# A PEER expert block: from one gathered and three dense token tiles to two and two, with dense products in plain f32

## What is computed

```python
qry = (h @ w_query).reshape(T, P_HEADS, 2, P_HALF)
scores = jnp.einsum("thcd,hcnd->thcn", qry, sub_keys).astype(jnp.float32)
s_top, i_top = lax.top_k(scores, P_TOPK)
...
gates = jax.nn.softmax(best_s, axis=-1).astype(h.dtype)
...
act = jax.nn.gelu(jnp.einsum("td,thkd->thk", hb, expert_u[eb]), approximate=False)
return jnp.einsum("thk,thkd->td", act * gb, expert_v[eb])
```

## Time and profile before

| | us |
|---|---|
| median of 3 runs | 1994.13 (1991.28 to 1994.95) |
| span of the profiled execution | 1990.5 |
| first u product | 822.9 |
| first fetch | 908.3 |
| u stage ends, v stage begins | about 1460 |
| last product | 1984.5 |

### The profile page before, as it was taken

One profiled execution on the slowest core, in us unless ns is written; L12 is line 12 of the kernel. 1 busy time (PEld: TensorE's weight loads), 2 busy tenths in 40 slices (PEclk: granted clock), 3 DMA queues, 4 the chain that ended last, 5 costly groups with the idle time before them and its releaser, 6 DMA issues.

```text
span 1990.5 us, 27945 instructions
## 1 busy us (share of the span) xinstructions
PE 1935.9 (97%) x10357; PEld 1710.3 (86%) x10357; DVE 1497.9 (75%) x2735; ACT 723.5 (36%) x1331; POOL 420.1 (21%) x231
## 2 busy tenths in 40 slices
PE   7999999999999999999999999999999999999998
PEld 4789777889877988999999999999988888888887
DVE  4776645364576537788889999996688898889986
ACT  4110233010351343343443444444444444444443
POOL 0333211444102023001111511111221222222210
PEclk9999999999999999999999999999999999999999
DMA  7235311353112432257668688888999999999993
GB/s 276 86 115 195 121 56 40 130 200 117 63 43 85 149 106 85 95 171 273 226 217 276 221 319 303 300 304 299 397 387 401 401 400 401 399 401 395 402 378 131
DMA packets 212644, 465.94 MB, mean 234 GB/s; under 512 B 15625, under 2 KB 157121, under 8 KB 193345
## 3 DMA queue, kind: packets, MB, share of 16 engines
q1 hardware_dynamic: 193408, 330.43, 47.7%
q0 software_dynamic: 18432, 134.23, 17.1%
q10 hardware_dynamic: 704, 0.04, 0.0%
HBM read 410.12 MB, written 54.53 MB: 233 GB/s over the span
## 4 chain that ended last, share of the span: by engine, by line
PE 43%; DMA 9%; DVE 4%; ACT 1%; issue 1%; SPq 1%; DVEq 0%; POOLq 0%; POOL 0%; ACTq 0%
PE xin_ps_u L2148 22%; PE xin_out L2192 16%; DMA experts_hot<-act_scratch 6%; PE xin_out L2170 4%; DMA con_raw<-in_expert_u 2%; DMA con_raw<-in_expert_v 1%; DVE over_v_vlo L2453 1%; DVE in_ulo L2304 1%; DVE experts_acc L1960 1%; SPq L2120 1%; DVE experts_rows L1941 1%; DVE xin_wt L2450 0%; ACT in_uhi L2221 0%; DVE xin_wlo L2455 0%; ACT L2263 0%
## 5 line engine op out<-in xcount | busy, mean ns | idle before, releaser
L1934 POOL DMA_INDIRECT experts_rows<-in_expert_rows,experts_idx x128 | 204.7, 1599 | 915.7 <-DVE experts_acc L1960 779.3
L2148 PE MATMUL xin_ps_u<-con_h_hi,in_uhi 128*128 128x384 f32 x1024 | 349.0, 341 | 11.3 <-DVE in_ulo L2304 9.1
L2148 PE MATMUL xin_ps_u<-con_h_hi,in_ulo 128*128 128x384 f32 x1024 | 343.3, 335 | 0.0
L2148 PE MATMUL xin_ps_u<-con_h_lo,in_uhi 128*128 128x384 f32 x1024 | 343.2, 335 | 0.0
L2192 PE MATMUL xin_out<-over_v_vhi,xin_whi 128*128 128x512 f32 x768 | 238.7, 389 | 2.3 <-DVE xin_wlo L2455 2.2
L2192 PE MATMUL xin_out<-over_v_vhi,xin_wlo 128*128 128x512 f32 x768 | 238.5, 389 | 0.0
L2192 PE MATMUL xin_out<-over_v_vlo,xin_whi 128*128 128x512 f32 x768 | 238.4, 389 | 0.0
L2304 DVE TENSOR_TENSOR in_ulo<-con_raw,in_uhi 128x1024 fp32r<-128x1024 f32 x127 | 155.2, 1222 | 81.2 <-ACT in_uhi L2221 78.7
L2148 PEld LDWEIGHTS xin_ps_u<-con_h_hi,in_uhi 128*128 128x128 f32 x1024 | 193.2, 189 | 15.6 <-DVE in_ulo L2304 13.0
L2148 PEld LDWEIGHTS xin_ps_u<-con_h_lo,in_uhi 128*128 128x128 f32 x1024 | 193.3, 189 | 0.0
L2148 PEld LDWEIGHTS xin_ps_u<-con_h_hi,in_ulo 128*128 128x128 f32 x1024 | 192.9, 188 | 0.0
(11 more groups left out here) (445 smaller groups left out, 3738.5 us busy)
## 6 DMA issues: line engine op xcount, KB each, us to landing
con_raw<-in_expert_u SPq DMA_DIRECT2D x128, 512.0 KB, 4.7
con_raw<-in_expert_v SPq DMA_DIRECT2D x128, 512.0 KB, 11.9
con_raw<-in_w_in SPq DMA_DIRECT2D x36, 1024.0 KB, 6.2
act_scratch<-in_act SPq DMA_DIRECT2D x128, 192.0 KB, 2.2
experts_hot<-act_scratch SPq DMA_DIRECT2D x128, 192.0 KB, 12.1
gate_scratch<-in_stage SPq DMA_DIRECT2D x12, 1024.0 KB, 7.2
gate_scratch<-over_s_stage SPq DMA_DIRECT2D x12, 1024.0 KB, 8.0
experts_hot<-gate_scratch SPq DMA_DIRECT2D x16, 768.0 KB, 14.0
```

Source lines behind the costliest of these rows:

```text
L1934: pool.indirect_dma_start(out=self.rows[:, r % ROWS, :], out_offset=None, in_=table, in_offset=at).then_inc(self.row_in[r % ROWS], 16)
L2148: mm = pe.matmul(ps_u[s % 2][:, 0:TD], a[s % 2][:, k, :], m[:, k, P:T], start=(i == 0), stop=(i == 3 * KD - 1))
```

## The change

It removes the dense work of tile 1 and gathers that tile too: 256 slots, first those of tile 0 and then of tile 1, with the same four row buffers. The dense part has tiles 2 and 3 (256 tokens).

- The dense products are plain f32: no rounded parts, no cuts on ACT and DVE, 8 matmuls of 256 columns in a u step (L2139), 4 of 512 in a v step (L2176).
- Activations and gates stay on the chip in `w` (128 KB in each partition). In 64 u steps from `S0` = 54 on, four tokens' gates are made in each: DVE makes one-hot rows times gate (`weighted_rows`), ACT the other one-hot rows from a distance (`distances`, `one_hot`), PE four products of 128 columns (L2159). Blocks still to come are filled by ACT (`keep_gates`), those that are done are multiplied by DVE (`gate_done_tiles`, L2424), and `gate_tile` (L2432) multiplies the new block's.
- Slot r is now `slot_work(r)`: the dot product of r, then the add of r-2. Slots start at step 18, two in three steps up to S0, one in each step after it. 98 are done in the u stage. The other 158 follow one another on DVE with no tie to PE's steps, the routing of tile 1 between the first twelve.
- The v stage reads `w` and the loaded block alone.
- Before it, `finish_block` also turns h of tile 1 back to rows and stores two row tiles to HBM; the v stage's first loads bring them back, and the residual rows with them.

The core of the diff; the helpers for routing only take other buffers:

```diff
-                for r in IN_AT[n - 1] if n else []:
-                    got.add(dve, r)
-                for r in IN_AT[n]:
-                    got.dot(dve, r, con.h0[:])
...
+def slots_of_steps():
+    at, r = [[] for n in range(NEXP)], 0
+    for n in range(FIRST_SLOT, NEXP):
+        if n >= S0 or (n - FIRST_SLOT) % 3 != 2:
+            at[n].append(r)
+            r += 1
+    return at
...
     def fetch(self, pool, r, table):
 
-        at = bass.IndirectOffsetOnAxis(ap=self.idx[:, r:r + 1], axis=0)
+        g, c = r // SLOTS, r % SLOTS
+        if c == 0:
+            pool.wait_ge(self.idx_done, g + 1)
+        at = bass.IndirectOffsetOnAxis(ap=self.idx[g][:, c:c + 1], axis=0)
         wait(pool, self.acc_done, r - ROWS + 1)
...
+            def products(n):
+                pe.wait_ge(ring.u_in[n % U_RING], 16 * (n // U_RING + 1))
+
+                wait(pe, gelu_done, n - 3)
+                wait(pe, w_in_place, placed(n - 4))
                 for k in range(KD):
-                    for a, m in ((uhi, hT[0]), (uhi, hT[1]), (ulo, hT[0])):
...
+                    mm = pe.matmul(ps_u[n % 4][:, 0:TD], u_of[n % U_RING][:, k, :], con.late[:, k, :], start=(k == 0),
+                                   stop=(k == KD - 1))
...
+            for n in range(NEXP):
+                pe.wait_ge(ring.v_in[n % U_RING], 16 * (n // U_RING + 1))
+                wait(pe, w_in_place, placed(n))
+                for t in range(ND):
+                    for h in range(2):
+                        mm = pe.matmul(out[t][h][:], w[:, n, t * P:(t + 1) * P], ring.tile[n % U_RING][:, h * 512:(h + 1) * 512],
+                                       start=(n == 0), stop=(n == NEXP - 1))
...
+            def weighted_rows(q):
+
+                dve.wait_ge(slots_done, 1 if q < N_HOT // 2 else 2)
+                wait(dve, g_done, q - 1)
+                for k in range(G_TOK):
+                    c = G_TOK * q + k
+                    op = dve.tensor_scalar(hot_i[q % 2][:, k, :], con.iota[:], slot[0][:, c:c + 1], slot[2][:, c:c + 1],
+                                           ALU.is_equal, ALU.mult)
+                op.then_inc(hot_i_done, 1)
...
+            def slot_work(r):
+                if r == SLOTS:
+                    dve.wait_ge(h1_in, 16)
+                got.dot(dve, r, rows_of(r))
+                if r == SLOTS + 2:
+                    dve.wait_ge(v_used, 12)
+                if r > 1:
+                    got.add(dve, r - 2)
...
+            for n in range(NEXP):
...
+                if group_of(n + 1) is not None:
+                    weighted_rows(group_of(n + 1))
+                if n > S0:
+                    gate_tile(n - 1)
+                for r in IN_AT[n]:
+                    slot_work(r)
+                if group_of(n) is not None:
+                    gate_done_tiles(group_of(n), n)
+            gate_tile(NEXP - 1)
+            for r in range(AFTER, 2 * SLOTS):
+                slot_work(r)
+                if r - AFTER < R_STEPS:
+                    route(3, r - AFTER)
```

More of the change, by code:

```diff
@@ L1531, in modulate, with keep_h @@
                                    bias=con.ada[:, 24 + k:25 + k], scale=con.scale_b[:, k:k + 1]).then_inc(modded, 1)
+            def keep_h(dst, t, half):
+                act.wait_ge(back, 2 * t + half + 1)
+                act.activation(dst[:, half * 512:(half + 1) * 512], ps_x[:], ACT.Copy).then_inc(h0_kept, 1)
             act.wait_ge(landed[1], base + 16)
@@ L1555, in _ @@
                     half = i - U + 3
-                    act.wait_ge(back, half + 1)
-                    act.activation(con.h0[:, half * 512:(half + 1) * 512], ps_x[:], ACT.Copy).then_inc(h0_kept, 1)
+                    keep_h(con.h0, 0, half)
             modulate(2)
+            act.wait_ge(ss2_done, NT - 1)
+            for half in range(2):
+                keep_h(h1, 1, half)
             square_tile(3)
@@ L1898, in _ @@
                     keep_scores(g - 1)
-                if g == PH - 2:
-                    act.wait_ge(ring.u_in[0], 16)
-                    act.activation(uhi[0][:], ring.tile[0].rearrange("p (k n) -> p k n", k=KD), ACT.Copy).then_inc(cut_hi, 1)
             keep_scores(PH - 1)
@@ new lines, in _ @@
+            sp.wait_ge(rt.searched, PH)
+            sp.dma_start(lists1, rt.lists[1]).then_inc(away, 16)
+            for n in range(U_RING, NEXP):
+                sp.wait_ge(u_done, n - 3)
+                ring.load_u(sp, A, n)
+            for n in range(NEXP):
+                if n < U_RING:
+                    sp.wait_ge(u_done, NEXP - 3 + n)
+                else:
+                    sp.wait_ge(v_used, n - 3)
+                ring.load_v(sp, A, n)
+                if n == 5:
+                    sp.dma_start(again, lists1).then_inc(again_in, 16)
+                if n == 11:
+                    sp.dma_start(h1, kept_rows[1]).then_inc(h1_in, 16)
+                if n == 19:
+                    sp.dma_start(row_b, kept_rows[0]).then_inc(row_b_in, 16)
+                if n >= 27 and n % 4 == 3 and n < 27 + 4 * NT:
+                    t = (n - 27) // 4
@@ new lines, in gates @@
+            def gates(q):
+                pe.wait_ge(hot_j_done, q + 1)
+                pe.wait_ge(hot_i_done, q + 1)
+                wait(pe, g_in_place, q - 1)
+                for k in range(G_TOK):
+                    mm = pe.matmul(ps_g[q % 2][:, k, :], hot_j[q % 2][:, k, :], hot_i[q % 2][:, k, :], start=True, stop=True)
+                mm.then_inc(g_done, 1)
+            for n in range(NEXP):
+                if group_of(n) is not None:
+                    gates(group_of(n))
+                products(n)
+                if n in (S0 - 4, S0 - 2):
+                    turn_slots(1 + (n - S0 + 4) // 2)
@@ new lines, in distances, with one_hot @@
+            def distances(q):
+                act.wait_ge(slots_done, 1 if q < N_HOT // 2 else 2)
+                wait(act, hot_j_done, q)
+                for k in range(G_TOK):
+                    c = G_TOK * q + k
+                    op = act.activation(distance[:, k, :], con.iota[:], ACT.Abs, bias=slot[1][:, c:c + 1], scale=-1.0)
+                op.then_inc(measured, 1)
+            def one_hot(q):
+                act.wait_ge(measured, q + 1)
+                wait(act, g_done, q - 1)
+                act.activation(hot_j[q % 2], distance, ACT.Relu, bias=con.ones[:, 0:1], scale=-1.0).then_inc(hot_j_done, 1)
@@ new lines, in square @@
+            def square(g):
+                act.wait_ge(got.acc_done, SLOTS * (g + 1))
+                act.wait_ge(v_used, 20)
+                wait(act, ss0_done, g)
+                act.activation(junk, got.acc[g], ACT.Square, accum_out=ss0[:, g:g + 1]).then_inc(ss0_done, 1)
+            for n in range(NEXP):
+                q = group_of(n + 1)
+                if q is not None:
+                    distances(q)
+                for r in IN_AT[n - 1] if n else []:
+                    got.weigh(act, r)
+                for o, s in ROUTE_AT[n]:
+                    if s == 3:
+                        exponents(o)
+                if q is not None:
+                    one_hot(q)
+                if group_of(n) is not None:
+                    keep_gates(group_of(n), n)
+                kept(n)
@@ new lines, in _ @@
+            for r in range(AFTER - 1, 2 * SLOTS):
+                got.weigh(act, r)
+                if r == AFTER + 3:
+                    exponents(3)
+                if r == FIRST_END:
+                    square(0)
+                if r == FIRST_END + 8:
+                    act.wait_ge(sum0_done, 1)
+                    act.dma_start(dst[0:P, :], x[:, 0]).then_inc(stored, 16)
+                if r == DENSE_END:
+                    for m in range(2 * ND):
+                        act.wait_ge(closed, m + 1)
+                        act.wait_ge(ss0_done, 1)
+                        wait(act, ss_done, m)
+                        act.activation(junk[:, 0:512], out[m // 2][m % 2][:], ACT.Square,
+                                       accum_out=ss[:, m:m + 1]).then_inc(ss_done, 1)
@@ L2299, in _, with at @@
         @block.vector
         def _(dve):
[L2301 to L2312 removed]
+            def at(o, k):
+                dve.wait_ge(chosen, STAGES * o + k)
@@ L2551, in build_program @@
+            for r in range(2 * SLOTS - 2, 2 * SLOTS):
+                got.add(dve, r)
+            for m in range(2 * ND):
+                add_half(m)
+            mean0(1)
+            scale0(1)
+            sum0(1)
 def build_program(nc, A, out):
```

837 lines of the change are left out of this document (343 added, 494 removed).

## The result

| | before | after |
|---|---|---|
| median of the runs, us | 1993.94 (4 runs, 1991.28 to 1994.95) | 2203.88 (4 runs, 2192.95 to 2207.23) |
| span of the profiled execution, us | 1990.5 | 2205.4 |

The ratio is 1.1045, 95% interval 1.1016 to 1.1073: slower by 210 us. The forecast was 2134 us in a range of 2030 to 2270. Sign and mechanism hold, the size was 70 us short.

What follows compares the result with a forecast made beforehand. The four-buffer gather ring was to bound the changed kernel: u stage to 1375 us, v stage to 1823, 69 leftover slots to 2120, 10 us of ending, span 2130, plus 3.6 over profile: 2134 us, range 2030 to 2270.

Steps and rivals of the forecast that it cites:

- What decides: Gather slots: fetch waits for the add, dot for its row; slots take 4.9 us in the u stage, PE idle at end.
- the same formula: Slot period with two fetches in flight: half of the fetch's landing time plus 2.9 us.
- Plain f32: PE's dense products: u step 3.44 us, 4.33 with gates, v step 3.46; dense work from 823 us on 940 instead of 1149.
- (a): Start of u stage to first gate step: 54 steps of 3.44 us, 186 us, ending at 1012 with table loads.
- (b): Rest of u stage: 74 steps with a slot each at the ring's 4.9 us, 363 us, ending at 1375.
- L: Time from a gather's issue to its landing: taken as 6.9 us in u stage, 7.2 in v stage, 5.7 alone.
- (c): The v stage: starts about 5 us later, takes 443 us, PE ends at 1823 with 89 slots done at 5.05 us.
- (d): Behind PE's end: 69 slots left at 4.3 us, 297 us, ending at 2120.
- (e): Behind the last add: half-tile adds, closing operations and a 0.5 MB store, 10 us, span 2130.
- POOL held off: Rival: DVE's one-hot instructions delay POOL's fetches in all 64 gate steps, adding 144 us, total 2278 us; chance 0.10.
- Bytes, not latency: Rival: a gather's landing shrinks to 3.6 us once nothing else is queued, total 1951 us; chance 0.05.

Runs made afterwards that it cites:

- Three orders of the same two operations: Changed kernel with add r-1 after the dot, 1961.2 us; add r-2 before the dot, 1973.6 us; add r-1 before the dot, 1949.2 us.
- one in flight: Changed kernel with the add one more slot behind, dot(r) then add(r-3), so one fetch is in flight: 3149.0 us.
- the versions above: Changed kernel with add(r-1) ahead of dot(r), 1949.2 us; the same with SP's routing-list store behind u tile 16's load, 1936.3 us.
- the version with the store later: Changed kernel with add(r-1) ahead of dot(r), plus SP's store of routing lists moved behind the load of u tile 16: 1936.3 us.

## Why the prediction was right, and where it was short

The mechanism was right and the total 3% short. Step by step, with the sum of the forecast against the profiled 2205.4 us (75 us above its 2130):

- **What decides.** Right. The fetch waits for the add, the dot for the row, PE stands idle at the end. Three orders of the same two operations and one in flight follow the same formula.
- **Plain f32.** Right: 4.36 us a gate step where nothing holds it (4.33 said), v stage 440 us (443 said).
- **(a) Start of the gate steps.** 1040 against 1012, a step that failed by omission. 10.0 us are the fifth u load, which stands behind SP's store of the routing lists. The forecast's "two stores on SP" are those of the two row tiles; the store of the lists, with its wait for the whole search, is nowhere in its sum. 12.1 us are the slot tables of the dense tiles, late because DVE's slots wait for rows ahead of the routing. Both waits vanish or fall to 0.6 us in the versions above. 2.9 us are the first u product, at 825.9 and not 823. The last 3 us are no wait: the 54 steps take 192.2 us beside the two waits, where the forecast has 189 with its table loads and the version with the store later takes 188.0, and the granted clock reads 0.92 and 0.95 in the first two windows above, where that version reads 1.00: part of these steps ran at the lower of its two levels.
- **(b) Gate and last u steps.** 368 us against 363. L was 7.9 and not 6.9 and the period 5.25 and not 4.9; but PE closes its last u step when 70 more slots are done, not 74, since nothing on PE waits for the last ones: 70 x 5.25 = 368. Two errors, nearly even.
- **(c) The v stage.** The term that was mis-sized. L was taken as 7.2, "nearer the u stage's row"; it is 8.2 to 8.6, next to the other bound, 8.9. The period is 5.6 and not 5.05: 79 slots and not 89. With three fewer before it (95, not 98), 174 are done at PE's end and not 187. I had reasoned from the mean rate (346 GB/s, 360 said). But beside the same v loads one gather in flight lands after 6.5 us and two after 8.6 (the table above): the second gather is the load that counts, and the row from which I took 6.9 had one at a time (seven fetches in 105 us).
- **(d) Behind PE's end.** L = 5.7 was right, the period 4.18 against 4.3. The gather that it was read from was less alone than the forecast says: SP issued other transfers from 1368.8 on, 2.3 us after its fetch, so the value held with some luck. But 82 slots are left and not 69: 348 us (1848.3 to 2196.4) against 297. That is 51 of the 75 us; 25 come from PE's later end.
- **(e)** 9 us against 10.
- **POOL held off.** Refuted: the fetch takes 0.94 us in the gate steps (shortest to longest of the 62 that start there), beside TENSOR_SCALARs that take 0.36 us each and not 0.22.
- **Bytes, not latency.** Refuted for this kernel, whose queues are at 0.71 behind PE's end, with a landing of 5.7 us and not 3.6. Bytes become the bound of the v stage as soon as three fetches are in flight.

## What to carry to other kernels

In a ring of buffers count the transfers that are in flight while the consumer waits: period = (landing + work between the landing and the release)/that number. A release that can be done ahead of a wait belongs ahead of it: here that swap alone is worth 230 us. Before a ring's demand is doubled, compare its ceiling, with the landing of the new load, to the new demand, and look in every queue at what stands behind a new wait, however short its own work.
